# A one-core hybrid decoder step: the order of work at the seams of its two feed-forward stages

## What is computed

```python
h = x + 0.5 * rmsnorm(swiglu(rmsnorm(x, ffn1_pre), ffn1_w_in, ffn1_w_out), ffn1_post)
u = rmsnorm(h, mix_pre);  P = u @ w_in            # feeds attention and the gated delta rule
merged = sigmoid(gate_a) * branch_a + sigmoid(gate_b) * branch_b
h = h + rmsnorm(merged @ w_o, mix_post)
y = h + 0.5 * rmsnorm(swiglu(rmsnorm(h, ffn2_pre), ffn2_w_in, ffn2_w_out), ffn2_post)
# swiglu(x): gate, up = split(x @ w_in);  (silu(gate) * up) @ w_out,   hidden width 2816
```

## Time and profile before

| | |
|---|---|
| median of 3 runs | 3644.06 us (3643.88 to 3648.87) |
| the profiled execution | 3643.35 us, its span 3641.5 us |
| PE matmul busy | 3465.7 us, 95% of the span |
| DVE, ACT, POOL busy | 2014.2 (55%), 1493.2 (41%), 770.0 us (21%) |
| DMA | 372.72 MB, mean 102 GB/s |
| granted PE clock, mean | 0.98 of full |
| matmuls L2752 + L2762 + L2774, in the chain that ended last | 10.7% + 6.5% + 0.7% of the span |

### The profile page before, as it was taken

How to read it: one execution, slowest core, us unless ns; L and a number is a source line. 1 busy time by engine, 2 the same in 40 slices (tenths; PEclk the granted TensorE clock), 3 DMA queues, 4 the chain that set the end, 5 groups by cost and what they waited for, 6 DMA issues and landing times. The chain is left out here.

```text
span 3641.5 us, 65166 instructions
## 1 busy us (share of the span) xinstructions
PE 3465.7 (95%) x25152; PEld 3289.1 (90%) x25152; DVE 2014.2 (55%) x3415; ACT 1493.2 (41%) x3083; POOL 770.0 (21%) x621
## 2 busy tenths in 40 slices
PE   8999989989999999989999999998999899998998
PEld 7999989988898888777988989997899799998998
DVE  7655556745554555543566566567432665555555
ACT  5222235635544555433344444344322632223444
POOL 3323201102222221000333223333000323231000
PEclk9999999999999999999999999999999999999999
DMA  4223246721212213793011111012332322223664
GB/s 160 84 71 89 71 146 212 224 86 54 66 63 83 62 60 96 256 370 128 20 37 36 42 42 39 22 31 78 127 93 77 107 74 86 74 86 111 202 194 137
DMA packets 343926, 372.72 MB, mean 102 GB/s; under 512 B 20980, under 2 KB 252222, under 8 KB 343502
## 3 DMA queue, kind: packets, MB, share of 16 engines
q1 hardware_dynamic: 334694, 339.49, 29.7%
q0 software_dynamic: 8880, 29.21, 2.2%
q10 hardware_dynamic: 84, 0.35, 0.0%
HBM read 297.42 MB, written 71.55 MB: 101 GB/s over the span
## 5 line engine op out<-in xcount | busy, mean ns | idle before, releaser
L657 PE MATMUL ps<-p_hi,w_hi 128*128 128x352 f32 x912 | 305.5, 335 | 3.4 <-PEq L120 1.5
L657 PE MATMUL ps<-p_hi,w_lo 128*128 128x352 f32 x912 | 294.5, 323 | 0.0
L657 PE MATMUL ps<-p_lo,w_hi 128*128 128x352 f32 x912 | 293.9, 322 | 0.0
L1923 PE MATMUL ps<-p_hi,w_hi 128*128 128x352 f32 x768 | 258.5, 337 | 0.0
L1923 PE MATMUL ps<-p_hi,w_lo 128*128 128x352 f32 x768 | 254.0, 331 | 0.0
L1923 PE MATMUL ps<-p_lo,w_hi 128*128 128x352 f32 x768 | 253.9, 331 | 0.0
L2762 PE MATMUL ps<-f_hid_hi,w_hi 128*128 128x352 f32 x528 | 172.0, 326 | 12.0 <-DVE w_lo L2438 12.0
L2762 PE MATMUL ps<-op_hid_hi,w_hi 128*128 128x384 f32 (+1 forms) x528 | 171.3, 324 | 12.5 <-DVE w_lo L2438 12.5
L1859 POOL TENSOR_TENSOR dl_mk<-dl_lo_t,cst 128x512 f32<-128x512 f32 x112 | 164.3, 1471 | 80.7 <-PE ps L2077 55.9
L657 PEld LDWEIGHTS ps<-p_hi,w_hi 128*128 128x128 f32 x912 | 173.0, 190 | 6.0 <-issue 3.0
L657 PEld LDWEIGHTS ps<-p_lo,w_hi 128*128 128x128 f32 x912 | 173.1, 190 | 0.0
(11 more groups left out here) (675 smaller groups left out, 10958.0 us busy)
## 6 DMA issues: line engine op xcount, KB each, us to landing
w_raw<-in_ffn_w_out_dram SPq DMA_DIRECT2D x136, 256.0 KB, 3.1
w_raw<-in_w_in_dram SPq DMA_DIRECT2D x67, 512.0 KB, 3.9
sa_v<-in_cache_v_dram SPq DMA_DIRECT2D x120, 256.0 KB, 6.7
w_raw<-in_ffn_w_in_dram SPq DMA_DIRECT2D x48, 512.0 KB, 4.9
sa_k<-in_cache_k_dram SPq DMA_DIRECT2D x72, 256.0 KB, 5.6
f_s<-in_ffn_w_out_dram SPq DMA_DIRECT2D x64, 256.0 KB, 3.2
pair_s<-in_ffn_w_out_dram SPq DMA_DIRECT2D x64, 256.0 KB, 3.1
d_hid<-f_gb SPq DMA_DIRECT2D x44, 264.0 KB, 2.1
```

What stands on the lines that cost most here:

```text
L657: mm = nc.tensor.matmul(m.ps[:, bank, 0:CH], a[:, k, w], b[:, f, cols(c)], start=(f == 0 and i == 0), stop=(f == KT - 1 and i == 2))
L1923: mm = nc.tensor.matmul(m.ps[:, (k + c) % 2, 0:CH], a[:, k, f * P:(f + 1) * P], x[:, f, cols(c)], start=(j == 0), stop=(j == len(terms) - 1))
```

## The change

1. **Seam, both stages.** `EARLY` takes tiles 0 to 9 into the product part instead of 0 to 15. Tiles 10 to 21 are split in steps 0 to 11 of pass 0, each behind the unit of its step instead of ahead of it. SP loads tiles 0 to 9, stores half 0 of tile 21, loads 10 to 13, stores half 1, and then loads one unit and one hidden tile in turn.
2. **Start of FFN2.** `t_values` takes one f at a time: f = 0, 1, 2 each ahead of one gate chunk, f = 3 between gate and up. FFN1 keeps its order.
3. **End of FFN1.** The eight matmuls of the last sum of squares go in two halves of four, after the second and the third of the four product chunks, instead of all behind the fourth. `next_unit(2, ..)` starts when the first half of its low parts is there and waits for the second ahead of f = 4.
4. **Rows of y.** PE turns at steps 17, 18 and 21 instead of 15, 16 and 18; ACT copies at 18, 19 and 21 instead of 16, 17 and 18.

No operation is added or taken away but for the waits.

```diff
--- before.py
+++ after.py
@@ -2295,17 +2295,16 @@
 
-    def t_values(dve):
-        for f in range(HALF):
-            dve.wait_ge(e.y2, f + 1)
-            nc.vector.scalar_tensor_tensor(out=t_val[:, N3, f, :], in0=x_quarter(0, 1, f), scalar=gain(0, f), in1=t_val[:, N4, f, :],
-                                           op0=ALU.mult, op1=ALU.subtract).then_inc(e.n3, 1)
-            dve.wait_ge(e.n3, f + 1)
-            nc.vector.scalar_tensor_tensor(out=t_val[:, T2, f, :], in0=x_quarter(0, 0, f), scalar=gain(0, f), in1=t_val[:, N3, f, :],
-                                           op0=ALU.mult, op1=ALU.subtract).then_inc(e.t2, 1)
-            dve.wait_ge(e.t2, f + 1)
-            nc.vector.scalar_tensor_tensor(out=t_val[:, N4, f, :], in0=x_quarter(1, 0, f), scalar=gain(1, f), in1=t_val[:, T2, f, :],
-                                           op0=ALU.mult, op1=ALU.subtract).then_inc(e.n4, 1)
+    def t_values(dve, f):
+        dve.wait_ge(e.y2, f + 1)
+        nc.vector.scalar_tensor_tensor(out=t_val[:, N3, f, :], in0=x_quarter(0, 1, f), scalar=gain(0, f), in1=t_val[:, N4, f, :],
+                                       op0=ALU.mult, op1=ALU.subtract).then_inc(e.n3, 1)
+        dve.wait_ge(e.n3, f + 1)
+        nc.vector.scalar_tensor_tensor(out=t_val[:, T2, f, :], in0=x_quarter(0, 0, f), scalar=gain(0, f), in1=t_val[:, N3, f, :],
+                                       op0=ALU.mult, op1=ALU.subtract).then_inc(e.t2, 1)
+        dve.wait_ge(e.t2, f + 1)
+        nc.vector.scalar_tensor_tensor(out=t_val[:, N4, f, :], in0=x_quarter(1, 0, f), scalar=gain(1, f), in1=t_val[:, T2, f, :],
+                                       op0=ALU.mult, op1=ALU.subtract).then_inc(e.n4, 1)
 
@@ -2466,7 +2465,8 @@
 
-    EARLY = {2: range(0, 3), 3: range(3, 6), 4: range(6, 9), 5: range(9, 13), 6: range(13, 16)}
+    EARLY = {2: range(0, 3), 3: range(3, 6), 4: range(6, 8), 5: range(8, 10)}
+    BEFORE = 10
 
@@ -2486,19 +2486,19 @@
             load_unit(sp, u)
-        for n in range(13):
+        for n in range(BEFORE):
             load_hid(sp, n)
         store_h(sp, FT - 1, 0)
-        for n in range(13, 16):
+        for n in range(BEFORE, BEFORE + 4):
             load_hid(sp, n)
         store_h(sp, FT - 1, 1)
-        for n in range(16, FT):
-            load_hid(sp, n)
         for h in range(6):
...
                     load_unit(sp, u + 8)
+                if h == 0 and BEFORE + 4 + k < FT:
+                    load_hid(sp, BEFORE + 4 + k)
                 if h in (1, 3):
@@ -2539,10 +2539,10 @@
                 u = h * FT + k
-                if h == 0 and k < FT - 16:
-                    hid_high(act, 16 + k)
                 if u + 3 < 6 * FT:
                     unit_high(act, u + 3)
+                if h == 0 and BEFORE + k < FT:
+                    hid_high(act, BEFORE + k)
                 if h in (1, 3) and k > 0:
@@ -2664,10 +2664,10 @@
                 u = h * FT + k
-                if h == 0 and k < FT - 16:
-                    hid_low(dve, 16 + k)
                 if u + 3 < 6 * FT:
                     unit_low(dve, u + 3)
+                if h == 0 and BEFORE + k < FT:
+                    hid_low(dve, BEFORE + k)
                 if h in (1, 3) and k > 0:
@@ -3179,7 +3179,8 @@
                                            in1=m.cst[:, C_POS:C_POS + 16], op0=ALU.mult, op1=ALU.add).then_inc(lam_there, 1)
-            e.t_values(dve)
+            for f in range(HALF):
+                e.t_values(dve, f)
             e.low(2, 0)
@@ -3338,20 +3339,25 @@
             def sum_h(c):
-                if c < 2:
-                    pe.wait_ge(h_pooled, 3 * c + 3)
-                    pe.wait_ge(e.y_copied, KT * c + 6)
-                n = 2 if c < 2 else KT
-                for f in range(n):
-                    if c == 2:
-                        pe.wait_ge(h_squared, 4 + f // HALF + 1)
-                    mm = nc.tensor.matmul(m.ps[:, 5, 0:CH], m.cst[:, C_MEAN:C_MEAN + P], acc[:, f, :], start=(f == 0), stop=(f == n - 1))
+                pe.wait_ge(h_pooled, 3 * c + 3)
+                pe.wait_ge(e.y_copied, KT * c + 6)
+                for f in range(2):
+                    mm = nc.tensor.matmul(m.ps[:, 5, 0:CH], m.cst[:, C_MEAN:C_MEAN + P], acc[:, f, :], start=(f == 0), stop=(f == 1))
                 mm.then_inc(h_summed, 1)
 
+            def sum_last_h(a):
+                pe.wait_ge(h_squared, 4 + a + 1)
+                for f in range(HALF * a, HALF * (a + 1)):
+                    mm = nc.tensor.matmul(m.ps[:, 5, 0:CH], m.cst[:, C_MEAN:C_MEAN + P], acc[:, f, :], start=(f == 0), stop=(f == KT - 1))
+                if a == 1:
+                    mm.then_inc(h_summed, 1)
+
             def next_unit(c, n):
-                pe.wait_ge(u_lo, KT * (c + 1) if c < 2 else 2 * KT + 2)
+                pe.wait_ge(u_lo, KT * (c + 1) if c < 2 else 2 * KT + 1)
                 pe.wait_ge(next_lo, n + 1)
                 for f in range(KT):
+                    if c == 2 and f == HALF:
+                        pe.wait_ge(u_lo, 2 * KT + 2)
                     w = slice(f * P, (f + 1) * P)
@@ -3377,9 +3383,10 @@
             next_unit(0, 1)
+            sum_last_h(0)
             next_unit(1, 0)
+            sum_last_h(1)
             next_unit(1, 1)
-            sum_h(2)
             pe.wait_ge(e.y_logged, 3)
@@ -3670,8 +3677,10 @@
                         e.root_y(act, h // 2 - 1, 4)
-                    elif k in (16, 17, 18):
-                        row(3 * (h // 2 - 1) + k - 16)
+                    elif k in (18, 19):
+                        row(3 * (h // 2 - 1) + k - 18)
+                    elif k == 21:
+                        row(3 * (h // 2 - 1) + 2)
 
@@ -3764,7 +3773,10 @@
             e.low(3, 1)
-            e.t_values(dve)
+
+            def rooted_chunk(c):
+                e.t_values(dve, c)
+                dve.wait_ge(rooted, 3 + c + 1)
 
@@ -3788,7 +3800,7 @@
             e.acc_free = acc_free
-            e.vector(dve, lambda c: dve.wait_ge(rooted, 3 + c + 1), lambda: None, during)
+            e.vector(dve, rooted_chunk, lambda: e.t_values(dve, HALF - 1), during)
             for a in range(2):
@@ -3928,11 +3940,11 @@
                         e.sum_y(pe, c, 4)
-                    elif k == 15:
+                    elif k == 17:
                         turn(3 * c)
-                    elif k == 16:
+                    elif k == 18:
                         turn(3 * c + 1)
-                    elif k == 18:
+                    elif k == 21:
                         turn(3 * c + 2)
```

## The result

| | before | after |
|---|---|---|
| median | 3645.69 us (3643.88 to 3648.87, 4 runs) | 3598.96 us (3596.61 to 3611.0, 4 runs) |
| ratio, 95% interval | 1 | 0.9878 [0.9854, 0.9901] |
| profiled execution, its span | 3643.35, 3641.5 us | 3598.97, 3597.3 us |
| PE matmul busy | 3465.7 us, 95% | 3461.8 us, 96% |

The forecast was 3600.7 us. The changed kernel is faster by about 1.2%.

What follows compares the result with a forecast made beforehand. PE, busy 95% of the span, was taken as the bound: only its idle stretches can go. Gains of 11.9, 11.7, 12.2, 6.3 and 1.3 (43.4) off 3643.35 give 3599.95, the median 0.7 higher: 3600.7 us; range 3594 to 3613.

Steps and rivals of the forecast that it cites:

- What bounds the kernel: Whole kernel: PE is busy 95% of the span, so only its idle stretches can go.
- the sum: Gains at five places, less new stalls and half clock: 43.4 us, giving 3600.7 us.
- the chain in the prediction: Both seams: two round trips through memory stand in front of unit 3; PE waits 12.2 and 12.0 us.
- DVE's further queue: Start of FFN2: `t_low`, gate 1, up 1 and units keep their sum and end, while PE comes 12 us sooner.
- price of a miss, under 1 us: Start of FFN2: cost if units 0 to 2, due 1, 0.5 and 0.1 us ahead of their products, come late.
- The term: Start of FFN2: gate wait 10.4 plus half clock 2.4 less a stall of 0.6, a gain of 12.2 us.
- DVE becomes the bound: FFN2, chance 0.06: f = 1 and 3 operations take 1.65, not 0.77; 3.5 us late, PE waits: 3604.
- a toss: End of FFN1: half clock may come or not, 0 to 5 us; taken as 1.1 against 2.2 before.
- The two new waits: FFN2's rows of y: ACT's late copy of the third row stalls the next pass, 0.6 and 0.8 us.
- The rival of small gaps: Chance 0.08: stalls of 1 to 2 us halve the clock; four places lose some 2 us each: 3609.
- The range: Whole kernel: 3594 us without the stalls and tail half clock, to 3613 with rivals at 3609 and some of both.

Runs made afterwards that it cites:

- e5_swap_only: Kernel before with only unit and hidden tile exchanged in each step, 16 early tiles kept; one execution, 3641.2 us.
- e3_tail_only: Kernel before with only the end of FFN1 changed (last sum of squares in halves); 3631.2 us, ratio 0.9978.
- e1_seam_only: Kernel before with only the seams changed (fewer early tiles, unit ahead of hidden tile, SP's order); 3615.1 us, ratio 0.9932.
- e2_start_only: Kernel before with only the start of FFN2 changed (`t_values` one f at a time between gate chunks); 3633.0 us, ratio 0.9984.
- e9_pad48: Changed kernel with 48 no-ops at the head of PE's queue, which never reached the chip; 3606.4 us, ratio 0.9894.
- e10_warm_pad: Changed kernel with 24 unread matmuls at the end of FFN1, plus 208 no-ops that never reached the chip; 3624.9 us, ratio 0.9942.
- e12_after_again: Changed kernel unaltered, run again on a chip where the kernel before took 3643.94 us; 3603.1 us, ratio 0.9888.
- the four parts alone: Four kernels, each the kernel before with one part of the change; gains by medians 24.4, 6.5, 8.3, 1.3 us, together 40.5.

## Why the prediction was right, and where it was not

*What bounds the kernel, and the seams.* Right in mechanism and size: 12.0 against 11.7 for FFN1, 13.1 against 13.2 for FFN2 with the rows. The stalls left were 1.3 and 1.1 (0.8 and 0.3) where the sum had 2.0 and 1.6. `e5_swap_only` shows that the exchange of unit and hidden tile alone is not enough, as the chain in the prediction said; the other half alone was not run.

*Start of FFN2.* The gate did what was forecast: the chunks on DVE kept 0.5 us beside POOL, and no gate wait is left. The step that failed is the sentence that DVE's further queue has an unchanged sum and ends where it did, "price of a miss, under 1 us". It added up DVE's durations as they stood in the old schedule, where POOL's subtractions came behind them. The change moved ACT's high parts forward, and with them POOL onto DVE: 4.5 us more on DVE, 2.8 us of wait for PE, and half clock behind it. The term was 12.2 and measured 8.4; with POOL held back it measured 11.9 (451.1 to 439.2). The prediction had weighed the shared access for `t_values` and for the gate, and not for the `t_low` operations behind them. The rival "DVE becomes the bound" had the right place and about the right price (3.5), for another reason: the operations of f = 1 and 3 took 0.77 as I had put them.

*End of FFN1.* Idle 4.3 us, near the 4.2 forecast. The sum had taken the half clock as a toss, at 1.1 us; it came: the 50 matmuls of the rows from 782 to 793 took 3.18 + 7.00 us, at 0.16 each they would have taken 8.0, so 2.2 for it and 5.1 instead of 6.3 in all (6.1 in `e3_tail_only`). This is the other term that was mis-sized. It was no toss in the end: in all seven profiles that have this idle piece of 4.3 us the clock fell behind it.

*Rows of y.* The two new waits are 1.7 together (1.4 forecast), the wait removed 2.7: 1.0 by the waits; the stretch (0.7) varies by more than that between kernels whose rows are the same.

*The rival of small gaps.* I had set it aside because of one wait of 2.7 us, whose row ends 0.5 us behind it. The clock did stay at 1.00 after it, but that does not carry over. The same wait of the same line, 2.7 us, comes in four kernels more: behind it the clock stayed in `e5_swap_only` and fell in `e1_seam_only`, `e2_start_only` and `e3_tail_only`. And the trace of the kernel before had a shorter wait behind which it fell, 1.75 us of L3289 up to 38.4 us. First the wait in `e3_tail_only` and the 4 us from its end, then the 4 us behind the wait of L3289 in the kernel before:

```profile
3555.12 1.97 PE L3918 MATMUL ps<-cst,acc_chunk 128*128 128x128 f32 x8 [2.70 <-DVE acc_chunk L3781]
...
3555.10:3559.10 4.00, 3.98 (x21) 3.98 (x22) 1.17 (x2) 0.00 (x0) 0.00 (x0) 0.62 0.43 149
```

```profile
38.40:42.40 4.00, 4.00 (x21) 3.96 (x22) 3.28 (x3) 3.11 (x7) 3.20 (x1) 0.65 0.63 270
```

In the changed kernel the clock fell behind the wait of 2.8 us of L2752, and did so in all seven profiles that have this wait (2.1 to 2.9 us). In `e9_pad48`, the same program, the seam of FFN1 had a stall of 1.8 us and half clock behind it, where the profile of the changed kernel had 1.3 and none:

```profile
503.85 0.43 PE L2762 MATMUL ps<-f_hid_hi,w_hi 128*128 128x352 f32 x1 [1.79 <-DVE w_lo L2437]
```

```profile
500.00:506.00 6.00, 4.21 (x21) 3.91 (x21) 4.47 (x8) 3.06 (x6) 0.00 (x0) 0.85 0.64 175
```

Its output part took 260.3 us instead of 258.3. `e10_warm_pad` had 1.9 us there, the clock fell too, and it took 260.3; in seven profiles with 1.0 to 1.4 us it did not fall (257.9 to 258.6). So short gaps do cost some 2 us each, in some executions and places. Of its four places the rival was right about the start of FFN2; its 3609 did not come, as the seams kept the full clock in most profiles.

*The sum.* By the stretches the change is worth 38.6 us, 4.8 less than forecast, and it is the untouched stretches that made up for it in the profiled execution. Three profiles of the same changed program have spans of 3597.3, 3596.1 and 3603.4 us and middle stretches (sample attention and delta rule) of 1090.9, 1088.9 and 1093.2. On the chip of `e12_after_again` the medians differ by 40.5 (3643.94 against 3603.4 over eight runs), near what the stretches say and as much as the four parts alone; on the chip of the result by 46.7. The range held; the closeness of the centre is partly luck.

## What to carry to other kernels

When two things are split on one engine in turn, the one whose data is already there must not be queued behind the one that still has a trip through memory to make. Here that order alone gave a third of the gain; the rest came with fewer tiles due early, whose own round trip no longer stood in front of the unit. When an edit moves an engine's work forward, price it with the neighbours it will have at its new time: a duration read beside an idle POOL is not the duration beside a busy one. A new kernel version should be compared stretch by stretch, since with instructions added in one stage a loop a thousand microseconds later took 28 us longer.

## What the runs showed of the hardware that I had not expected

- With 24 added matmuls (48 instructions of PE) ahead of a hardware loop, PE stood at each of the loop's four jumps back: 8 waits, 15.0 us, 37 more packets of instructions, and with the half clock behind each pair 23 us in the loop. The twelve profiles without them had 180 or 181 packets, the two with them 217.
- DVE's subtractions of 128x528 took 0.70 us each by themselves and 1.83 where they met POOL's; POOL's took 1.33 and 1.79. The engines then went in turn, one start of each every 1.75 us.
- The same wait of 2.7 us was followed by full clock in two profiles and by a fall in three. Gaps of 1.8 and 1.9 us at the seam of FFN1 brought half clock, gaps of 1.0 to 1.4 there did not; 24 matmuls in a gap of 4.3 kept the full clock.
